# A two-block transformer kernel: the first stage in another order, with the second x tile in two pieces, the tables loaded later and one set of column sums left to TensorE

## The chip, the cores and the metric

The kernel runs on one core of one Trainium2 chip. The metric is the device time of one execution in microseconds (us), as the median of several runs. One more execution is recorded by the profiler; all rows shown are from it.

## The reference, cut to what matters

Two transformer blocks run in a row on 256 tokens of width 2048, in fp32. What the change touches is the start of the first block: the modulation vector, the normed and modulated x, and its product with `w_in`.

```python
cs = jax.nn.silu(c)
mod = cs @ w_ada[l] + b_ada[l]
sh1, sc1, gt1, sh2, sc2, gt2 = [m[:, None, :] for m in jnp.split(mod, 6, axis=-1)]
h = _rmsnorm(x, g_pre_mix[l]) * (1.0 + sc1) + sh1
proj = h @ w_in[l]
p_moba, p_dsa, p_qi, p_ki, p_wi, ga, gb = jnp.split(proj, split_pts, axis=-1)
...
x = x + gt1 * _rmsnorm(y, g_post_mix[l])
h = _rmsnorm(x, g_pre_ffn[l]) * (1.0 + sc2) + sh2
f = jnp.square(jax.nn.relu(h @ w_ff1[l])) @ w_ff2[l]
x = x + gt2 * _rmsnorm(f, g_post_ffn[l])
```

`h` can't be made before the column sums over all 2048 rows of `w_ada` for its columns (`sh1`, `sc1`) are there. The second block (attention with dilated windows and latent attention, then its own feed-forward part) has no modulation and isn't touched.

## The kernel before, in words

**Numbers as pairs.** Every weight is split into a high part `wh` (ScalarE, a copy that rounds, L1307) and a low part `wl` (VectorE, weight minus high part, L1678); `h` is kept as high and low halves in `HT`. One 128x512 product is then three matmuls: high x high (L983), low x high (L984), high x low (L986).

**Chunks.** Weights stream from HBM in the order of `plan()`, one DMA for each event (L930, on SyncE's queue), into seven raw buffers in this stage. An event "g" is a chunk: two rows of 128 of a slab 1024 columns wide. A chunk gives two pieces; `wh` and `wl` have a ring of four pieces, so two chunks. TensorE works a chunk as four banks (ps0 to ps3: two token tiles by two column halves) of six matmuls each, 24 in all.

**Phases.** `h` has 16 column tiles (k = 0 to 15). Six slabs (qi, qB, kB, vB, kA, vA) are run three times, over k 0 to 3, then 4 to 8, then 9 to 15 (`PHASES`). A slab of phase 0 is copied out of PSUM by ScalarE (L1601), one of phase 1 is added by VectorE (L2011). Phase 0 has 12 chunks, called c0 to c11 below, phase 1 has 18.

**Modulations.** Tiles 0, 1 (the first pair) and 2, 3 (the second pair) come from events "p": four events of 1 MB each for a pair, with 256 columns of shift and 256 of scale for four of the 16 rows. TensorE sums the shift columns of such a piece directly (`row_vec`, four matmuls with one output row, L1043), VectorE the scale columns (four operations, L1696 and L1699). After a pair's fourth piece ScalarE copies TensorE's row out (L1353), `column_sums` turns both into columns (L1055, L1058), VectorE forms the modulation `AV` (L1704 to L1711), and `x_halves` writes the two `HT` tiles (ScalarE L1360, VectorE L1761, L1764). The columns for the later phases come as events "s", whose sums VectorE does alone (L1696, L1699); after the last one `column_sums` (L1067) and the tasks "turnx" follow, which scale two tiles of x (ScalarE L1346), turn them (TensorE L1102), apply the modulation (ScalarE L1333, L1337) and make the low half (VectorE L1751).

**Order.** `work_order()` writes one list of items that all engines follow; each engine takes its own kinds from it, in that order. In it the first pair's four sums, its tiles, the second pair's sums and chunk c0 (qi, k 0 and 1) are written by hand; from c1 on `run()` goes through the slabs: the sums of the events behind a chunk, the split of the next chunk, then the four banks. A "rot" task (sines and cosines from the table in `CT`, L1868 to L1900) runs in five parts on VectorE between the first chunks.

**Loads.** SyncE's queue brings the vectors, both token tiles of x (1 MB each) and then the stream; GpSimd's queue brings at the start the constants `CT` (identity and tables, 376 KB), the positions and a mask (192 KB).

```python
def x_norm():
    for t in range(2):
        e.wait_ge(x_landed[t], 16)
```

Of the kernel before, what the change touches and what calls it, by code (L numbers as in the profile page):

```python
# [15 lines left out]
D = 2048  # L16
# [70 lines left out]
def plan():  # L87
# [30 lines left out]
    out += [("p", 0, i) for i in range(4)] + [("p", 1, 0), ("p", 1, 1), chunks.pop(0), ("p", 1, 2), ("p", 1, 3)]  # L118
    beside(chunks, columns, (1, 2, 2, 1, 2, 2, 2, 2, 2, 1, 1))
    beside(phase(1), columns, (1, 1, 1, 1, 1, 1, 1, 1, 1, 1, 1, 1, 1, 1, 0, 0, 0, 0))  # L120
# [143 lines left out]
def work_order():  # L264
# [7 lines left out]
    def add(*item):  # L272
        items.append(item)
# [267 lines left out]
    def first_sums(*ns):  # L541
        for n in ns:
            ada(n)
            add("rowvec", n)
            if n == 0:
                add("xnorm")
                add("xturn", 0)
                add("xturn", 1)

    first_sums(0, 1, 2, 3)  # L550
    add("rowcopy", 3)
    colsum(3)
    first_sums(4)
    add("xhalves", 0)
    split(6)
    first_sums(5, 7, 8)
    for t in range(2):
        for b in range(2):
            if (t, b) == (1, 1):
                add("rowcopy", 8)  # L560
                colsum(8)
            add("bank", "qi@0", parts[6], t, b, True, False)
    at["done"] = parts[6][-1]
    add("xhalves", 1)
    at["pos"] = 9
    later("rot")
    for q in range(2):
        for name in FIRST:
            if (name, q) == ("vA", 0):
                finish("rot")  # L570
            run(f"{name}@{q}", begin=1 if (name, q) == ("qi", 0) else 0)
# [69 lines left out]
def build(nc, stream, vecs, rows, consts, masks, x_in, pos_in, out):  # L641
# [32 lines left out]
    PB, PTB, FIRST_ROW = ACC[:, 1024:1408], ACC[:, 1408:1792], ACC[0:1, 512:768]  # L674
# [15 lines left out]
    vec_in, const_in, caus_in = sem("vec_in"), sem("const_in"), sem("caus_in")  # L690
    x_landed = [sem(f"x{t}_in") for t in range(2)]
# [218 lines left out]

    def x_part(p, t):
# [7 lines left out]
    def sync(e):  # L919
        e.dma_start(VT[:, :], vecs).then_inc(vec_in, 16)  # L920
        for t in range(2):
            e.dma_start(X[:, t, :], x_in[0, 128 * t:128 * t + 128, :]).then_inc(x_landed[t], 16)
        for n, (off, w) in enumerate(offs):
            i, _, m = place[n]
            if m >= 0:
                if events[m][0] == "p":
                    e.wait_ge(*rowvec(m))
                e.wait_ge(*read_last(m))
# [10 lines left out]
    def gpsimd(e):  # L939
        e.dma_start(CT[:, :], consts).then_inc(const_in, 16)  # L940
# [1281 lines left out]
```

## Time and profile before

| | |
|---|---|
| median of three runs | 2619.52 us (2616.36 to 2620.04) |
| the profiled execution | 2613.94 us, span 2612.1 us |
| TensorE busy | 2557.7 us of the span (98%) |
| VectorE, ScalarE busy | 1734.9 us (66%), 1206.0 us (46%) |
| HBM traffic | 216 GB/s over the span, 370 to 376 GB/s in the first 130 us |

The span is what the trace covers; the execution takes 1.8 us more. Busy time of TensorE is modelled from pipelined matmuls, so its idle gaps and the distance between matmul starts say more than its share. The change lies within the first 190 us, so the rows below are mostly of these. A row's bracket gives the engine's idle time before it and what ended that.

### The profile page before, as it was taken

The page shows a single profiled execution, that of the slowest core. Times are in us where ns is not written, and L with a number is a line of the kernel's source. Part 1 is how long each engine was busy: PE and PEld are TensorE (multiplying, and loading weights), DVE is VectorE, ACT ScalarE, POOL GpSimd, SP SyncE. Part 2 cuts the span into 40 slices and gives each one's busy share as a digit, 9 for nine tenths or more (in the row PEclk, how much of TensorE's full clock was granted, in tenths as well). Part 3 has the DMA queues.
Part 4 walks back from the last instruction along what each step waited for, and adds up shares of the span by engine and source line. Part 5 has one row for each costly group of instructions (what it writes and reads, how often), then busy time and mean ns, then how long its engine had stood idle before and what let it go on. Part 6 is the DMA issues. An engine that isn't in the chain of part 4 may idle for free.

```text
span 2612.1 us, 30557 instructions
## 1 busy us (share of the span) xinstructions
PE 2557.7 (98%) x12370; PEld 2115.0 (81%) x12370; DVE 1734.9 (66%) x2307; ACT 1206.0 (46%) x1737; POOL 5.9 (0%) x15
## 2 busy tenths in 40 slices
PE   7999998999999999999999999999999999999998
PEld 4887786887787888888888878878788888888887
DVE  6887878878887776556556564546665565564665
ACT  4534444533446434434434465455564343443443
POOL 0000000000000000000000000000000000000000
PEclk9999999999999999999999999999999999999999
DMA  9984345688885775555555545534545555555553
GB/s 376 375 330 170 121 159 210 265 339 327 338 329 205 292 280 207 199 187 188 199 179 192 195 169 183 189 126 146 185 169 193 181 190 195 188 196 194 178 193 145
DMA packets 80444, 567.11 MB, mean 217 GB/s; under 512 B 8976, under 2 KB 9104, under 8 KB 15664
## 3 DMA queue, kind: packets, MB, share of 16 engines
q1 hardware_dynamic: 79200, 558.09, 58.2%
q0 software_dynamic: 1104, 7.07, 0.7%
q8 instruction: 98, 1.61, 0.2%
q14 instruction: 42, 0.34, 0.0%
HBM read 563.02 MB, written 2.10 MB: 216 GB/s over the span
## 4 chain that ended last, share of the span: by engine, by line
PE 84%; DVE 10%; ACT 2%; DMA 2%; issue 1%; DVEq 0%; SPq 0%; ACTq 0%
PE ps L986 19%; PE ps L983 19%; PE ps L984 18%; PE ps L1027 16%; PE ps L1029 8%; DVE wl L1678 3%; DMA raw<-stream_in 2%; DVE ACC L1699 2%; ACT wh L1307 1%; PE ps L1247 1%; DVE TMP L1804 1%; DVE M L1808 1%; PE ps L1223 1%; DVE M L2011 0%; PE ps L1087 0%
## 5 line engine op out<-in xcount | busy, mean ns | idle before, releaser
L1678 DVE TENSOR_TENSOR wl<-raw,wh 128x1024 fp32r<-128x1024 f32 x845 | 996.7, 1220 | 566.7 <-ACT wh L1307 566.1
L1307 ACT ACTIVATE wh<-raw 128x1024 fp32r<-128x1024 f32 x845 | 846.8, 1049 | 723.3 <-PE ps L986 551.8
L1027 PE MATMUL ps<-HT,wh 128*128 128x512 f32 x1792 | 634.2, 399 | 0.0
L983 PE MATMUL ps<-wh,U 128*128 128x512 f32 x1376 | 538.2, 391 | 0.0
L986 PE MATMUL ps<-wl,U 128*128 128x512 f32 x1376 | 536.4, 390 | 1.3 <-DVE wl L1678 1.3
L984 PE MATMUL ps<-wh,U 128*128 128x512 f32 x1376 | 535.6, 389 | 0.0
L1029 PE MATMUL ps<-HT,wl 128*128 128x256 f32 x1792 | 503.5, 281 | 0.6 <-DVE wl L1678 0.6
L983 PE MATMUL ps<-wh,HT 128*128 128x512 f32 x1096 | 439.0, 401 | 7.7 <-DVE HT L2106 3.3
L986 PE MATMUL ps<-wl,HT 128*128 128x512 f32 x1096 | 432.8, 395 | 11.2 <-DVE wl L1678 11.1
L984 PE MATMUL ps<-wh,HT 128*128 128x512 f32 x1096 | 429.4, 392 | 0.0
L1027 PEld LDWEIGHTS ps<-HT,wh 128*128 128x128 f32 x1792 | 336.6, 188 | 82.7 <-DVE M L2048 0.2
L1029 PEld LDWEIGHTS ps<-HT,wl 128*128 128x128 f32 x1792 | 338.5, 189 | 2.0 <-DVE wl L1678 1.5
L986 PEld LDWEIGHTS ps<-wl,U 128*128 128x128 f32 x1376 | 258.3, 188 | 57.9 <-DVE wl L1678 3.9
L984 PEld LDWEIGHTS ps<-wh,U 128*128 128x128 f32 x1376 | 258.4, 188 | 53.1 <-issue 0.2
L983 PEld LDWEIGHTS ps<-wh,U 128*128 128x128 f32 x1376 | 258.3, 188 | 53.0 <-issue 0.2
L986 PEld LDWEIGHTS ps<-wl,HT 128*128 128x128 f32 x1096 | 207.1, 189 | 63.9 <-DVE wl L1678 20.1
L983 PEld LDWEIGHTS ps<-wh,HT 128*128 128x128 f32 x1096 | 207.5, 189 | 55.0 <-DVE HT L2106 4.5
L984 PEld LDWEIGHTS ps<-wh,HT 128*128 128x128 f32 x1096 | 207.6, 189 | 41.3 <-issue 0.5
L1699 DVE SCALAR_TENSOR_TENSOR ACC<-raw,VT,ACC 128x1024 f32<-128x1024 f32 (+3 forms) x180 | 222.7, 1237 | 5.0 <-DMA raw<-stream_in 0.9
L1617 ACT ACTIVATE M<-ps 128x256 f32<-128x256 f32 x112 | 43.1, 385 | 213.7 <-PE ps L1029 213.7
L1619 ACT ACTIVATE U<-M 128x256 fp32r<-128x256 f32 x112 | 46.8, 418 | 139.3 <-DVE M L2054 139.3
L2048 DVE TENSOR_TENSOR M<-ps,M 128x256 f32<-128x256 f32 x112 | 47.5, 424 | 61.6 <-ACT M L1617 61.1
(265 smaller groups left out, 1373.4 us busy)
## 6 DMA issues: line engine op xcount, KB each, us to landing
raw<-stream_in SPq DMA_DIRECT2D x497, 1024.0 KB, 4.8
raw<-stream_in SPq DMA_DIRECT2D x16, 896.0 KB, 7.4
raw<-stream_in SPq DMA_DIRECT2D x17, 640.0 KB, 6.2
raw<-stream_in SPq DMA_DIRECT2D x13, 512.0 KB, 4.8
M<-rows_in POOLq DMA_DIRECT2D x6, 1024.0 KB, 5.7
X<-x_in SPq DMA_DIRECT2D x2, 1024.0 KB, 7.0
y_out<-X SPq DMA_DIRECT2D x4, 512.0 KB, 2.7
CT<-consts_in POOLq DMA_DIRECT2D x1, 376.0 KB, 6.7
```

Of the source, the lines that this page charges most:

```text
L983: e.matmul(o, ah, H[:, c:c + bw], start=k == k0, stop=False)
L984: e.matmul(o, al, H[:, c:c + bw], start=False, stop=False)
L986: ins = e.matmul(o, ah, L[:, c:c + bw], start=False, stop=end)
L1027: e.matmul(o[:, :], H[:, c], a.rearrange("p h n -> p (h n)"), start=k == 0, stop=False)
L1029: ins = e.matmul(o[:, 0:256], L[:, c], a[:, 0, :], start=False, stop=k == 15)
L1223: e.matmul(bank[7][:, 0:256], att_in(A, "v", h, 0), PTB[:, 0:256], start=True, stop=False)
L1307: e.activation(H, raw[place[n][0]][:, c:c + w], ACT.Copy).then_inc(*hi.tick(p))
L1617: e.activation(z, bank[i % 4][:, 256:512], ACT.Copy).then_inc(*evac_a.tick((name, i)))
L1619: e.activation(d[:, 0, :], z, ACT.Copy).then_inc(*high.tick(key))
L1678: e.tensor_tensor(L, raw[place[n][0]][:, c:c + w], H.bitcast(F32), ALU.subtract).then_inc(*lo.tick(p))
L1699: e.scalar_tensor_tensor(a, r, cs, a, ALU.mult, ALU.add).then_inc(*acc.tick(key))
L2048: e.tensor_tensor(z, p[:, 0:256], z, ALU.add).then_inc(*evac_v.tick((name, i)))
```

## The change

1. **Slab order.** qi@0 holds only k 0 and 1 (one chunk), and qi@1 holds k 2 to 8. So phase 0 has 11 chunks and phase 1 has 19. The chunk of qi@0 is streamed before the second pair's modulations, and qB's first chunk between their second and third piece. Below, c0, c1, ... are the chunks in their order in the kernel at hand, with 24 matmuls each in phase 0 in both.
2. **Hand-written start.** The new list puts c0's four banks and c1's first banks between the second pair's row sums. `x_halves` is done half by half across both engines: the tiles lie in two banks (ps5, ps6), so that ScalarE reads one while VectorE reads the other.
3. **x in pieces.** Token tile 0 of x comes first, tile 1 in two pieces of 512 KB behind the third and the fourth stream event; each tile has its own squares, root and reciprocal.
4. **Tables late.** GpSimd's queue loads only the identity (128 of 752 columns of `CT`) at the start, and the rest and the mask after the second pair's last row sum. VectorE's rot and rope wait for `table_in`.
5. **One piece by TensorE alone.** For event ("p", 1, 0) TensorE sums all 512 columns, and VectorE none; `column_sums` adds that part.
6. **Columns.** The 32 "s" events are spread otherwise: 16 over phase 0's chunks c2 to c10, 16 over phase 1's first 16 chunks (before: 18 and 14).

```diff
+SLABS["qi@0"], SLABS["qi@1"] = (*SLABS["qi"][:3], 0, 2), (*SLABS["qi"][:3], 2, PHASES[2])
...
-    out += [("p", 0, i) for i in range(4)] + [("p", 1, 0), ("p", 1, 1), chunks.pop(0), ("p", 1, 2), ("p", 1, 3)]
-    beside(chunks, columns, (1, 2, 2, 1, 2, 2, 2, 2, 2, 1, 1))
+    out += [("p", 0, i) for i in range(4)] + [chunks.pop(0), ("p", 1, 0), ("p", 1, 1), chunks.pop(0), ("p", 1, 2), ("p", 1, 3)]
+    beside(chunks, columns, (1, 2, 2, 2, 2, 2, 2, 2, 1))
...
+    add("xsquare", 0)
+    add("xnorm", 0)
+    for n in range(3):
+        sums(n)
...
+    add("xsquare", 1)
+    sums(3)
+    add("xsquare", 2)
     add("rowcopy", 3)
...
+    add("xturn", 0)
+    split_piece(4, 0, only=("ACT",))
     add("xhalves", 0)
...
+    add("bank", "qi@0", parts[4], 0, 0, True, True)
+    evac("qi@0", 0, 0)
+    sums(5, False)
+    add("bank", "qi@0", parts[4], 0, 1, True, True)
+    add("xturn", 1)
+    evac("qi@0", 0, 1)
+    sums(6)
+    split(7)
...
+    add("bank", "qB@0", parts[7], 0, 0, True, False)
+    for n in (8, 9):
+        sums(n)
+    add("rowcopy", 9)
...
+    def both_by_pe(n):
+
+        return events[n] == ("p", 1, 0)
...
-        for t in range(2):
-            e.dma_start(X[:, t, :], x_in[0, 128 * t:128 * t + 128, :]).then_inc(x_landed[t], 16)
+        e.dma_start(X[:, 0, :], x_in[0, 0:128, :]).then_inc(x_landed[0], 16)
         for n, (off, w) in enumerate(offs):
+            if n in (3, 4):
+                a = slice(1024 * (n - 3), 1024 * (n - 3) + 1024)
+                e.dma_start(X[:, 1, a], x_in[0, 128:256, a]).then_inc(x_landed[n - 2], 16)
...
-        e.dma_start(CT[:, :], consts).then_inc(const_in, 16)
+        e.dma_start(CT[:, 0:C_COS], consts[:, 0:C_COS]).then_inc(const_in, 16)
         e.dma_start(POS[:, :], pos_in).then_inc(pos_landed, 16)
+        e.memset(ONES[:, :], 1.0).then_inc(ones_set, 1)
+        e.wait_ge(*rowvec(9))
+        e.dma_start(CT[:, C_COS:C_N], consts[:, C_COS:C_N]).then_inc(table_in, 16)
...
+                w = 512 if both_by_pe(n) else 256
```

**First place, TensorE behind the first pair.** ps4 takes the row sums (`L1043` before, `L1081` now), ps5 and ps6 the turned x, ps0 to ps3 the chunk's banks. Before, right behind the first pair's column sums:

```order
L1058 MATMUL ps7<-ONES,ACC 128x1 x2
L1043 MATMUL ps4<-raw4,VT 1x256 x4
L1043 MATMUL ps4<-raw5,VT 1x256 x4
L1043 MATMUL ps4<-raw0,VT 1x256 x4
L1043 MATMUL ps4<-raw1,VT 1x256 x4
L983 MATMUL ps0<-wh0,HT 128x512
```

The same place now, from the last turned tile of the first pair:

```order
L1148 MATMUL ps6<-CT,RT 128x128
L1019 MATMUL ps0<-wh0,HT 128x512
L1020 MATMUL ps0<-wh0,HT 128x512
L1022 MATMUL ps0<-wl0,HT 128x512
L1019 MATMUL ps0<-wh1,HT 128x512
L1020 MATMUL ps0<-wh1,HT 128x512
L1022 MATMUL ps0<-wl1,HT 128x512
L1081 MATMUL ps4<-raw5,VT 1x512 x4
L1019 MATMUL ps1<-wh0,HT 128x512
```

The first bank of c0 moved ahead of all four row sums of the second pair, and one of these is twice as wide. In what follows there (not shown) ps1, a turn of x, the next row sum, ps2, ps3, c1's ps0, two row sums, c1's ps1, the column sums and c1's ps2 and ps3 come in this order.

**Second place, ScalarE between phase 0 and phase 1.** `M<-ps` copies a bank out, QKT and RT take scaled x, `TMP<-ps5` and `TMP<-ps6` apply the modulation to a turned pair of tiles. Before, from the split of the last chunk of phase 0 (c11):

```order
L1307 ACTIVATE wh3<-raw1 128x1024
L1346 ACTIVATE QKT<-X,RS 128x256
L1346 ACTIVATE RT<-X,RS 128x256
L1333 ACTIVATE TMP<-ps5,AV 128x256 x2
L1337 ACTIVATE HT<-TMP 128x2x256
L1307 ACTIVATE wh0<-raw3 128x1024
L1307 ACTIVATE wh1<-raw3 128x1024
L1601 ACTIVATE M<-ps0 128x512
L1601 ACTIVATE M<-ps1 128x512
L1346 ACTIVATE QKT<-X,RS 128x256
```

Now, from the last copy of phase 0:

```order
L1654 ACTIVATE M<-ps3 128x512
L1394 ACTIVATE QKT<-X,RS 128x256
L1394 ACTIVATE RT<-X,RS 128x256
L1384 ACTIVATE TMP<-ps5,AV 128x256 x2
L1388 ACTIVATE HT<-TMP 128x2x256
L1394 ACTIVATE QKT<-X,RS 128x256
L1394 ACTIVATE RT<-X,RS 128x256
L1384 ACTIVATE TMP<-ps6,AV 128x256 x2
L1388 ACTIVATE HT<-TMP 128x2x256
L1355 ACTIVATE wh0<-raw2 128x1024
L1355 ACTIVATE wh1<-raw2 128x1024
L1394 ACTIVATE QKT<-X,RS 128x128
```

Two tiles' worth of work now stands in one piece behind phase 0's last bank. On TensorE (not shown) the column sums L1110 x10 and the eight turns L1148 into ps5 and ps6 stand directly behind that bank too, and ahead of the first bank of c11, the first chunk of phase 1; before, the ten column sums stood ahead of c10, the turns into ps5 in the middle of c10 and those into ps6 in the middle of c11.

## Rows read from the trace of the kernel before

**Rows 1.** Windows by stage; columns PE, PEld, DVE, ACT, POOL busy (x), clock, DMA, GB/s.

```profile
12.67:42.45 29.78, 25.73 (x113) 12.99 (x113) 21.15 (x49) 8.74 (x16) 0.00 (x0) 1.00 1.01 421
...
51.26:94.79 43.53, 43.53 (x194) 36.05 (x193) 42.55 (x45) 26.56 (x35) 0.00 (x0) 1.00 0.98 384
94.79:123.90 29.11, 27.72 (x135) 22.61 (x134) 21.55 (x22) 19.14 (x29) 0.00 (x0) 1.00 0.90 354
123.90:166.07 42.17, 41.93 (x184) 34.07 (x184) 42.17 (x37) 15.26 (x15) 0.00 (x0) 1.00 0.97 374
...
183.59:2612.10 2428.51, 2393.94 (x11638) 1989.21 (x11637) 1583.76 (x2124) 1119.06 (x1623) 3.73 (x7) 1.00 0.56 205
```

**Rows 2.** Timeline of the start (start, us, engine, line, operation, count, idle before).

```profile
6.55 1.91 ACT L1312 ACTIVATE M<-X 128x2048 f32<-128x2048 f32 x1 [3.70 <-DMA X<-x_in]
17.63 2.05 DVE L1699 SCALAR_TENSOR_TENSOR ACC<-raw,VT,ACC 128x256 f32<-128x256 f32 x4 [0.43 <-DMA raw<-stream_in]
23.23 0.37 ACT L1353 ACTIVATE ACC<-ps 1x256 f32<-1x256 f32 x1 [6.39 <-PE ps L1043]
27.57 2.00 ACT L1307 ACTIVATE wh<-raw 128x1024 fp32r<-128x1024 f32 x2 [1.20 <-DMA raw<-stream_in]
28.89 2.35 DVE L1678 TENSOR_TENSOR wl<-raw,wh 128x1024 fp32r<-128x1024 f32 x2
```

**Rows 3.** TensorE, fp32 matmuls: two pieces' row sums; ns min/median/max at 512 columns.

```profile
24.79 3.61 PE L1043 MATMUL ps<-raw,VT 128*1 128x256 f32 x16
...
L1075 PE MATMUL ps<-ACC,ONES x16: 590/592/595, 595.5 to 1003.4; 128*128 128x512 f32 x16
```

**Rows 4.** Timeline, ScalarE: the copy of c1's last bank.

```profile
51.46 0.60 ACT L1601 ACTIVATE M<-ps 128x512 f32<-128x512 f32 x1 [0.76 <-PE ps L986]
```

**Rows 5.** Timeline, VectorE between c2 and c5.

```profile
46.30 2.35 DVE L1678 TENSOR_TENSOR wl<-raw,wh 128x1024 fp32r<-128x1024 f32 x2
48.57 0.16 DVE L1868 CAST ST<-POS 128x2 f32<-128x2 int32 x1
...
50.70 3.21 DVE L1699 SCALAR_TENSOR_TENSOR ACC<-raw,VT,ACC 128x1280 f32<-128x1280 f32 x2
...
61.85 0.20 DVE L1878 TENSOR_SCALAR M<-M 128x96 f32<-128x96 f32 x1
...
63.34 1.55 DVE L1699 SCALAR_TENSOR_TENSOR ACC<-raw,VT,ACC 128x1280 f32<-128x1280 f32 x1
```

**Rows 6.** Timeline, three engines from phase 0 to phase 1.

```profile
94.79 2.29 PE L1067 MATMUL ps<-ONES,ACC 128*128 128x1 f32 x20
96.94 0.48 PE L983 MATMUL ps<-wh,HT 128*128 128x512 f32 x1
97.46 1.15 DVE L1696 TENSOR_SCALAR ACC<-raw,VT 128x1792 f32<-128x1792 f32 x1
...
106.39 0.50 ACT L1346 ACTIVATE QKT<-X,RS 128x256 f32<-128x256 f32 x1
106.94 0.33 PE L1102 MATMUL ps<-CT,QKT 128*128 128x128 f32 x1 [1.08 <-ACT QKT L1346]
107.92 1.02 ACT L1333 ACTIVATE TMP<-ps,AV 128x256 f32<-128x256 f32 x2 [0.64 <-PE ps L1102]
108.97 0.63 ACT L1337 ACTIVATE HT<-TMP 128x512 fp32r<-128x512 f32 x1
110.67 0.60 ACT L1601 ACTIVATE M<-ps 128x512 f32<-128x512 f32 x1 [0.58 <-PE ps L986]
```

**Rows 7.** Timeline: phase 1, first addition on VectorE; TensorE's last column sums.

```profile
123.90 2.48 DVE L2011 TENSOR_TENSOR M<-ps,M 128x512 f32<-128x512 f32 x4
...
180.55 3.18 PE L1067 MATMUL ps<-ONES,ACC 128*128 128x1 f32 x28
```

**Rows 8.** Window at the lower clock, columns as in rows 1.

```profile
44.50:47.90 3.40, 3.40 (x8) 2.47 (x9) 3.40 (x4) 1.24 (x2) 0.00 (x0) 0.54 0.72 251
```

**Rows 9.** DMA issues: KB, us to landing.

```profile
CT<-consts_in POOLq DMA_DIRECT2D x1, 376.0 KB, 6.7
```

More of the change, by code:

```diff
@@ L539, in ffn, with sums @@
                 later("srow", f)
[L541 to L550, printed above, removed]
+    def sums(n, dve=True):
+        if dve:
+            add("ada", n)
+        add("rowvec", n)
+    add("xsquare", 0)
+    add("xnorm", 0)
+    for n in range(3):
+        sums(n)
+    for p in range(2):
+        add("xq", p, 0)
+    add("xsquare", 1)
+    sums(3)
+    add("xsquare", 2)
     add("rowcopy", 3)
+    add("xnorm", 1)
+    add("xq", 0, 1)
     colsum(3)
-    first_sums(4)
+    add("xturn", 0)
+    split_piece(4, 0, only=("ACT",))
     add("xhalves", 0)
-    split(6)
-    first_sums(5, 7, 8)
-    for t in range(2):
[L558 to L563, printed above, removed]
-    add("xhalves", 1)
-    at["pos"] = 9
+    add("DVE", "split", parts[4][0])
+    split_piece(4, 1)
+    add("xq", 1, 1)
+    add("bank", "qi@0", parts[4], 0, 0, True, True)
[6 more added lines that the diff above has]
+    split(7)
+    for b in range(2):
+        add("bank", "qi@0", parts[4], 1, b, True, True)
+        evac("qi@0", 1, b)
+    at["done"] = parts[4][-1]
+    add("bank", "qB@0", parts[7], 0, 0, True, False)
+    for n in (8, 9):
+        sums(n)
+    add("rowcopy", 9)
+    add("bank", "qB@0", parts[7], 0, 1, True, False)
+    split_piece(10, 0)
+    colsum(9)
+    add("xhalves", 1)
+    split_piece(10, 1)
+    for b in range(2):
+        add("bank", "qB@0", parts[7], 1, b, True, False)
+    at["done"] = parts[7][-1]
+    at["pos"] = 10
     later("rot")
@@ L570, in work_order @@
                 finish("rot")
-            run(f"{name}@{q}", begin=1 if (name, q) == ("qi", 0) else 0)
+            if (name, q) != ("qi", 0):
+                run(f"{name}@{q}", begin=1 if (name, q) == ("qB", 0) else 0)
         flush()
@@ L1096, in x_turn @@
             e.wait_ge(const_in, 16)
-            for s, q in free[b]:
-                e.wait_ge(*s(q))
+            for q0 in ((5, 6) if p < 2 else (b,)):
+                for s, q in free[q0]:
+                    e.wait_ge(*s(q))
             for i in range(nk):
@@ L1352, in row_copy @@
             e.wait_ge(*rowvec(n))
[L1353 removed]
+            e.activation(FIRST_ROW[:, 0:w], bank[4][0:1, 0:w], ACT.Copy).then_inc(*copied.tick(("row", n)))
         def x_halves(p):
@@ L1364, in turn_x @@
         def turn_x(task, seg):
-            x_turn(task[1])
             k = X_TILES[task[1]][0]
+            e.wait_ge(*turned(("turnx", task[1] - 2)))
+            for t in range(2):
+                x_quarter(task[1], t)
             e.wait_ge(*mods(("av", 1, max(q for q in PHASES if q <= k))))
```

108 lines of the change are left out of this document (62 added, 46 removed).

## The prediction

> **What bounds the kernel now.** I read three views, in this order: the windows by stage, to see which engine is full in each; the timeline of the first 50 us, to see what TensorE waits for; and the timeline around the step from phase 0 to phase 1, where the order of work changes again.
>
> The windows [rows 1] show five stages. From 12.67 to 42.45 us TensorE has only 113 matmul records, and DMA is full (1.01) at 421 GB/s. From 51.26 to 94.79 both TensorE and VectorE are full (43.53 and 42.55 of 43.53 us) and DMA nearly (0.98). From 123.90 to 166.07 VectorE is busy for 42.17 of 42.17 us: it sets the pace there. After 183.59 TensorE is busy 2394 of 2429 us and VectorE 1584, and nothing in the change touches this part. So what counts is how much earlier or later TensorE stands at the same point of its work at about 184 us; that shift goes through to the end one to one.
>
> Units. The eight chunks c2 to c9 run from 51.26 us (c1's last copy starts at 51.46 [rows 4], about 0.2 us behind the bank's last start) to the column sums at 94.79 [rows 6]: 5.44 us a chunk, 0.227 us a matmul. A stream event of 1 MB takes 2.48 us: the third lands at 17.63, the seventh at 27.57 [rows 2], so the first landed at 12.67.
>
> **The start, until c2 begins.** Ahead of the first event x's second tile goes (1 MB, 2.48 us) and the tables and the mask (0.50 MB, 1.2 us), so it lands at 8.97. The fourth lands at 17.65 behind the first half tile, the second half tile at 18.9, c0's weights at 21.4, and the second pair's four pieces and c1's at 23.9, 26.3, 31.3, 33.8 and 28.8. Loads then run 1.2 us ahead of before, event for event.
>
> When does c0's first bank end? The half tile's squares take about 1.1 us (half of 1.91 [rows 2], and a read-out), so ScalarE copies the row at 20.05. Before, 5.66 us lay between that copy and the split of c0 (23.23 to 28.89), of which 2.0 were four sums that no longer stand between (2.05 for four [rows 2]); the turn of x is now inside the stretch (0.7, from 106.94 and what follows it in [rows 6]). So `wl` starts at 24.4, both pieces are there 2.27 us later (46.30 to 48.57 [rows 5]), and the first bank ends at 26.95. Bounds: 24.7 (c0's landing, one copy and the two splits, nothing else) and 29.
>
> From there TensorE has no wait that I can find until c2, since everything it needs has landed before its turn. It has 42 matmuls of c0 and c1 (9.5 us); three row sums at 1.71 (two take 3.4 without the tail of 3.61 [rows 3]); the wide row sum of the piece that it sums alone, 3.4; a turn, 0.7; six narrow column sums at 0.215 (ten take 2.15, from 94.79 to 96.94 [rows 6]), 1.3. The wide one isn't in the trace of before in this form: its lower bound is 1.71 (width free), the upper 4.7 (eight records one behind the other at the 592 ns of the fp32 matmul of 512 columns [rows 3]); I take 3.4, double width at double time, nearest to the narrow row that it widens. Sum: 20.0 us, so **c2 begins at 47.1 instead of 51.26, 4.2 us earlier**. 2.0 us of VectorE's work is saved for 1.7 of TensorE's, in a stretch where VectorE will wait (about 9 us between 28.8 and 44) and TensorE won't; the 1.7 is in the sum.
>
> **Phase 0.** VectorE finishes c2's split at about 48.0, and from there works in one piece. Its load per chunk is a split 2.27 and two columns 3.12 (the row at 50.70 has 3.21 with its tail [rows 5]), 5.39 against TensorE's 5.44, plus the rot parts: 2.13 behind c3's split (48.57 to 50.70 before), 1.49 in the third part (61.85 to 63.34), 0.2 for each small operation (61.85), so 0.4 in each of the others. Before, single columns at c1 and c4 made room for these; now there is one, 0.8 us for the first form. From 48.0: 0.8; split, rot, two columns 7.52; 5.75; 6.88; and 1.13 for the first half of c6's split: 70.1. TensorE wants it at 47.1 + 4 x 5.44 + 0.46 = 69.3. So 0.8 late, and 0.3 more at c7 and at c8, each behind a small rot part: **1.4 us given back**. Phase 0's 11 chunks end at T = 47.1 + 9 x 5.44 + 1.4 = 97.5.
>
> **From phase 0 to phase 1.** Here two tiles of x are now made in a row with no chunk between. Column sums take until T+2.15; the modulation is there at T+2.7 (96.94 to 97.46), ScalarE's two applications and copy end at T+4.4 (1.02 + 0.63), only then comes the scaling for the second tile, and TensorE's turn starts 0.55 later (106.39 to 106.94 [rows 6]) and ends at T+5.65: c11 starts. The second tile's application starts 1.53 behind its scaling (106.39 to 107.92), T+5.9, and ends at T+7.6; ScalarE then does c12's two copies, 2.0 (27.57 [rows 2]), and the third tile's scaling, so the turn in the middle of c11 is at T+10.1, when its first two banks are done since T+8.4. c12 starts at T+13.1 = 110.6. Before, c12 started at 110.47 (110.67 less 0.2) with the third tile's turn, 0.6, still in front; c13 at 116.5 against 116.0 now. So **of 2.8 us left, 2.3 go here** and 0.5 stay.
>
> **Phase 1.** VectorE's cadence is 42.17 / 3 = 14.06 us a slab [rows 1]: five splits, three columns, four additions from 123.90 on [rows 7]. TensorE needs 60 x 0.227 = 13.6. The 0.5 us is kept through three slabs. But kA's slab had two columns before, its column sums coming at 180.55 [rows 7], and has three now: a fourth slab at VectorE's pace, 0.45 slower. The column sums (about 3 us) are the same and only one chunk later; the turns behind them have 5 us and more of chunks each in front of their use. **Shift at the end: 0.1 us earlier, so none.**
>
> Costed at nothing: the tables late (0.50 MB in a stretch where the loads are ahead: c4's weights land about 46, ScalarE takes them at 53; rival three has the price), the pieces of x (one more reduction and one more addition on VectorE while it waits), the two-bank `x_halves` (its saving of half a us is within the bounds of the first bank).
>
> The profiled execution took 2613.94 us, its span 2612.1 and 1.8 around it; less 0.1 it is 2613.8. The median shown is 5.6 above the profiled one, so the forecast on its scale is **2619.4**.
>
> **Rival one, the start's gain goes through.** If the boundary costs what it cost before, and phase 0 keeps TensorE's pace, 4.2 less 0.45 stay: 2615.8. For it: VectorE is idle for 8.6 of the 29.78 us up to 42.45 and for 7.6 of the 29.11 behind 94.79 [rows 1], so there is slack on both sides of phase 0. Against it: ScalarE's order puts two tiles behind phase 0's last bank, and TensorE's turn waits for the second's scaling. A part of it is likelier than all.
>
> **Rival two, the low clock (slower).** In 44.50 to 47.90 the granted clock was 0.54 and TensorE started 8 matmuls in 3.4 us [rows 8], 0.425 apiece, which is the 1.2 GHz level; such a stretch costs 1.6 us. It came behind a gap at the end of c0. Now the gap there is gone, which is in my 4.2. But the first bank of c0 stands between waits at 22 to 27 us, and the boundary has a wait of 2.8 us behind narrow column sums. One stretch at the boundary costs nothing, as the third tile's turn leaves TensorE 1.7 us idle inside c11. In the start it costs 1.6 each, up to three (each followed by new waits on narrow sums): 2621.1 for one, 2624.3 for three; from the fourth the change is slower by over 0.2%.
> The Trainium skill (TensorE: Matmul & The Clock Gate, Part 4: PE-mode transpose) says that turns on TensorE don't count as busy for the clock as other matmuls do. By that rule the eight turns ahead of c11 make the low stretch there near certain; the sum would be the same, as it lies in c11. No row here shows it.
>
> **Rival three, the tables come too late (slower).** Their load waits for the last row sum, about 41.7. Before, 376 KB took 6.7 us from issue to landing [rows 9] among full queues; so 48.4, and VectorE needs them behind c3's split at 51.1: 2.7 us of cover. If they take twice as long (13.4), VectorE stands still for 4.0 us in a stretch where it sets the pace: 2623.4; slower than before from about 9.5 us on.
> The Trainium skill (SBUF — State Buffer, section "A bandwidth-pool intuition that's wrong") says a load from GpSimd's queue can be held up by VectorE operations that take the shared port, and gives 3.1 us for one that takes 0.6 alone. With 2.5 us more the tables would land at 50.9, just in time, and the sum would stand.
>
> **How the numbers follow.** No change, within 1.5 us of 2619.4: 0.50. Rival one in part or whole, 2615 to 2618: 0.27. Rival two: 0.17. Rival three: 0.06. The start's bounds (first bank 24.7 to 29, wide sum 1.7 to 4.7) move c2 by 4 us down and 3.4 up, but phase 0 and the boundary give most of it back in the same way; half of it I count at the end. Medians of three here spread by 1 to 2 us besides. The range is 2614.0 to 2623.5. A change of 0.2% is 5.2 us, about what a measurement of this kernel can tell from none. Faster by more needs rival one whole and the low stretch or the first bank at its bound too: 0.06. Slower by more needs three to four low stretches or very late tables: 0.07. So 0.87 for the same.
>
> **What would show it.** In the profile of the changed kernel: c0's first matmul at about 24 and c2's at 47; VectorE idle for 8 to 9 us between 28 and 44; TensorE waiting for `wl` at c6 by under 1 us; a wait of TensorE of about 2.5 us for ScalarE's scaling (QKT or RT, L1394) near 100 us and one of about 1.6 near 107; VectorE's first addition (L2074) at 123.4; the second column sums about at the same time as before plus one chunk. I am wrong if c11 starts before 101 us, if VectorE isn't the full engine in phase 1, or if a clock of 0.5 shows before 47 us.

## The result, and the profile after

| | kernel before | changed kernel |
|---|---|---|
| median | 2617.74 us (20 runs, 2614.53 to 2622.59) | 2622.22 us (20 runs, 2619.03 to 3191.05) |
| the profiled execution | 2613.94 us, span 2612.1 | 2621.33 us, span 2619.5 |

The change makes the kernel slower: ratio 1.0015, 95% interval 1.0008 to 1.0022, so about 4 us. One run of 3191.05 us was disturbed and is left out of the ratio. The forecast was "no change" (0.1 us earlier) at 2619.4 us. The time lies in its range, but the step is small and real: the interval's lower end is above 1.

The windows of the changed kernel (columns: PE, PEld, DVE, ACT, POOL busy with counts, clock, DMA share, GB/s). The first four are stages, laid out like those of [rows 1]: the start up to the end of c0's first bank, phase 0 from c2 on, the step between the phases (from the column sums behind c10 to VectorE's first addition), and three slabs of phase 1.

```profile
9.61:28.25 18.64, 14.48 (x50) 5.98 (x50) 13.55 (x32) 7.95 (x16) 0.00 (x0) 0.91 1.01 423
49.51:100.85 51.34, 50.43 (x217) 40.09 (x216) 49.19 (x58) 29.66 (x40) 0.00 (x0) 1.00 0.94 366
100.85:127.16 26.31, 24.09 (x111) 19.59 (x110) 17.21 (x17) 14.99 (x23) 0.00 (x0) 0.87 0.84 323
127.16:169.34 42.18, 41.95 (x184) 34.08 (x184) 42.18 (x38) 15.26 (x15) 0.00 (x0) 1.00 0.96 364
24.80:28.20 3.40, 3.15 (x6) 1.59 (x6) 3.33 (x6) 0.69 (x2) 0.00 (x0) 0.50 1.01 422
103.30:110.10 6.80, 4.58 (x15) 3.33 (x13) 1.97 (x6) 5.13 (x10) 0.00 (x0) 0.50 0.65 268
192.10:198.90 6.80, 6.80 (x21) 5.53 (x21) 1.54 (x4) 0.00 (x0) 0.00 (x0) 0.50 0.43 142
```

The last three rows are stretches at the low clock: 0.50 of 2.4 GHz is the 1.2 GHz level. In the trace of before there was one such stretch from 20 to 180 us [rows 8] and one of 3.4 us behind the last column sums, at 184.7. Now there is one over c0's first bank, one over the step between the phases, and one of 6.8 us behind the last column sums.

The timeline of the start and of c6 (start, us, engine, operation, idle before), to be laid beside [rows 2, 4]. L1019, L1020 and L1022 are the three matmuls of a product, L1081 the row sums:

```profile
19.69 1.06 ACT L1361 ACTIVATE M<-X 128x1024 f32<-128x1024 f32 x1 [2.70 <-DMA X<-x_in]
24.78 0.79 PE L1019 MATMUL ps<-wh,HT 128*128 128x512 f32 x1 [1.93 <-DVE HT L1827]
24.98 2.35 DVE L1733 TENSOR_TENSOR wl<-raw,wh 128x1024 fp32r<-128x1024 f32 x2
28.25 3.59 PE L1081 MATMUL ps<-raw,VT 128*1 128x512 f32 x8
39.93 3.61 PE L1081 MATMUL ps<-raw,VT 128*1 128x256 f32 x16
49.51 0.39 PE L1019 MATMUL ps<-wh,HT 128*128 128x512 f32 x1
72.83 0.50 PE L1022 MATMUL ps<-wl,HT 128*128 128x512 f32 x1 [0.71 <-DVE wl L1733]
```

c2 begins at 49.51, 1.75 us earlier than the 51.26 before. The step between the phases, to be laid beside [rows 6]:

```profile
100.85 2.29 PE L1110 MATMUL ps<-ONES,ACC 128*128 128x1 f32 x20
103.18 0.17 DVE L1759 TENSOR_TENSOR AV<-ps,VT 128x5 f32<-128x5 f32 x1 [3.24 <-PE ps L1110]
103.92 1.02 ACT L1384 ACTIVATE TMP<-ps,AV 128x256 f32<-128x256 f32 x2 [1.48 <-DVE AV L1766]
105.50 0.49 ACT L1394 ACTIVATE QKT<-X,RS 128x256 f32<-128x256 f32 x1
106.05 0.47 PE L1148 MATMUL ps<-CT,QKT 128*128 128x128 f32 x1 [2.22 <-ACT QKT L1394]
107.00 0.78 PE L1019 MATMUL ps<-wh,HT 128*128 128x512 f32 x1
127.16 2.48 DVE L2074 TENSOR_TENSOR M<-ps,M 128x512 f32<-128x512 f32 x4
```

T, the start of the column sums behind phase 0, is 100.85, c11 starts at 107.00, and VectorE's first addition comes at 127.16 instead of 123.90 [rows 7]. A wait of TensorE for an addition, 1.4 us long and at the same point of the work in every kernel here, serves as a mark near 300 us:

```profile
297.01 0.50 PE L983 MATMUL ps<-wh,HT 128*128 128x512 f32 x1 [1.39 <-DVE M L2011]
```

```profile
302.69 0.50 PE L1019 MATMUL ps<-wh,HT 128*128 128x512 f32 x1 [1.39 <-DVE M L2074]
```

The first is the kernel before, the second the changed one: 5.7 us late. Behind it the order of work is the same in both. The spans differ by 7.4 at the end; the other 1.7 is one stretch of low clock at 1943 us that only the second trace has. Such stretches vary from run to run (next section).

### The profile page after: what moved, and what is told of

Same layout as the page of the kernel before. It is cut to its first block, busy times and chain, and to the rows that moved or that the text cites. A ratio compares the mean times of both kernels' runs of the same rounds, so it can differ in the third digit from the quotient of the medians.

```text
span 2619.5 us, 30569 instructions
## 1 busy us (share of the span) xinstructions
PE 2567.7 (98%) x12374; PEld 2118.1 (81%) x12374; DVE 1733.4 (66%) x2306; ACT 1206.1 (46%) x1740; POOL 6.4 (0%) x16
## 4 chain that ended last, share of the span: by engine, by line
PE 85%; DVE 10%; ACT 2%; issue 1%; DMA 1%; SPq 0%; DVEq 0%; ACTq 0%
PE ps L1022 19%; PE ps L1019 19%; PE ps L1020 19%; PE ps L1063 16%; PE ps L1065 8%; DVE wl L1733 3%; DVE ACC L1754 2%; ACT wh L1355 1%; PE ps L1295 1%; DMA X<-x_in 1%; DVE TMP L1867 1%; DVE M L1871 1%; PE ps L1271 1%; DVE M L2074 1%; PE ps L1110 0%
## 5 line engine op out<-in xcount | busy, mean ns | idle before, releaser
L1019 PE MATMUL ps<-wh,U 128*128 128x512 f32 x1376 | 538.2, 391 | 0.0
L1022 PE MATMUL ps<-wl,U 128*128 128x512 f32 x1376 | 536.4, 390 | 1.4 <-DVE wl L1733 1.4
L1020 PE MATMUL ps<-wh,U 128*128 128x512 f32 x1376 | 535.5, 389 | 0.0
L1019 PE MATMUL ps<-wh,HT 128*128 128x512 f32 x1096 | 440.2, 402 | 8.7 <-DVE HT L2169 3.3
L1022 PE MATMUL ps<-wl,HT 128*128 128x512 f32 x1096 | 433.7, 396 | 10.7 <-DVE wl L1733 10.7
L1020 PE MATMUL ps<-wh,HT 128*128 128x512 f32 x1096 | 430.6, 393 | 0.0
L1022 PEld LDWEIGHTS ps<-wl,U 128*128 128x128 f32 x1376 | 258.3, 188 | 57.8 <-DVE wl L1733 3.8
L1020 PEld LDWEIGHTS ps<-wh,U 128*128 128x128 f32 x1376 | 258.4, 188 | 53.3 <-issue 0.2
L1019 PEld LDWEIGHTS ps<-wh,U 128*128 128x128 f32 x1376 | 258.3, 188 | 52.9 <-issue 0.2
L1022 PEld LDWEIGHTS ps<-wl,HT 128*128 128x128 f32 x1096 | 207.6, 189 | 66.4 <-DVE wl L1733 22.5
L1019 PEld LDWEIGHTS ps<-wh,HT 128*128 128x128 f32 x1096 | 208.0, 190 | 57.4 <-DVE M L2074 4.9
L1020 PEld LDWEIGHTS ps<-wh,HT 128*128 128x128 f32 x1096 | 208.0, 190 | 41.2 <-issue 0.5
```

Of the source, the lines that this page charges most:

```text
L1019: e.matmul(o, ah, H[:, c:c + bw], start=k == k0, stop=False)
L1020: e.matmul(o, al, H[:, c:c + bw], start=False, stop=False)
L1022: ins = e.matmul(o, ah, L[:, c:c + bw], start=False, stop=end)
```

## The experiments

Twelve kernels were measured in three groups of four, each group on a chip of its own and together with the kernel before. The first group is the two same kernels again, one_tile and fill_boundary; the second fill_start, no_wide, spread and tables_early; the third light_fill and the three combinations. Times are medians; the kernel before had 2617.69 in the first group, 2618.28 in the second, 2618.05 in the third. Within a group medians can be set side by side. Between groups only the ratios to the kernel before can, and a difference of 0.001 (2.6 us) between two ratios is about what their intervals leave open. So the times say whether a kernel is faster than the one before, and the traces what one part of it cost.

### The same two kernels again

No edit.

> The changed kernel once more, for its clock: if the low stretches (24.8 to 28.2, 103.3 to 110.1, 192.1 to 198.9, two near 440, one at 1943 us) belong to the order of work, the first three stand in the same places again and last as long; if they are chance, they move or change in number. Time 2622 in either case, 0.15% over the kernel before.

> The kernel before once more, for its clock: low stretches at 44.5 to 47.9 and 184.6 to 188.0 again if they belong to the order of work, each 3.4 us long; ratio 1.000.

The changed kernel: 2621.74 us, ratio 1.0015 (1.0006 to 1.0024). The kernel before: 2615.90, ratio 0.9996 (0.9985 to 1.0006). Windows of the changed kernel's second trace, then of the other's:

```profile
24.40:31.70 7.30, 6.05 (x11) 2.12 (x12) 5.24 (x9) 2.31 (x4) 0.00 (x0) 0.55 1.01 422
105.90:113.30 7.40, 5.80 (x16) 4.54 (x17) 3.44 (x4) 6.05 (x12) 0.00 (x0) 0.54 0.46 189
193.90:198.00 4.10, 4.10 (x17) 3.32 (x17) 1.54 (x4) 0.00 (x0) 0.00 (x0) 0.61 0.22 48
```

```profile
44.70:48.20 3.50, 3.16 (x8) 2.44 (x8) 3.50 (x5) 1.58 (x3) 0.00 (x0) 0.52 0.68 231
```

The places belong to the order of work; the lengths don't. In the start the low clock lasted 3.4 us in one trace and about 7 in the other, and behind the last column sums 6.8 and 3.4. Further stretches, near 430, 450, 720 or 1940 us, come and go in both kernels.

The execution of the second trace of the kernel before took 2623.78 us, 10 more than that of the first, though it had passed the mark at 297.49, only 0.5 later. About 3 of the 10 are two more stretches of low clock (at 434 and 1946 us). Most of the rest, 6 to 7 us, is not the clock: near 730 us weights came late in this trace and TensorE waited for them. The first row is the trace before at this place, the second the later one; clock 1.00 in both, DMA share 0.99 and 0.73:

```profile
722.00:734.00 12.00, 12.00 (x57) 9.91 (x56) 11.46 (x11) 4.62 (x5) 0.00 (x0) 1.00 0.99 373
728.00:742.00 14.00, 11.31 (x44) 7.50 (x43) 10.56 (x9) 4.50 (x5) 0.00 (x0) 1.00 0.73 245
```

Why they came late isn't shown. So shifts are read at the mark and verdicts from the timed runs.

### The step between the phases: one_tile

```diff
-        finish("turnx", X_TILES.index((PHASES[q + 1], 2)))
+        if q:
+            finish("turnx", X_TILES.index((PHASES[q + 1], 2)))
```

> The changed kernel, but at the step from phase 0 to phase 1 only the column sums stand between c10 and c11; the turns of the two x tiles come in the middle of c11 and of c12, as in the kernel before (the work is the same, only its place). Theory W (the wait for ScalarE's scaling, 2.2 us, and the turns behind it, not covered by any chunk, are what the boundary costs, and what runs slowly behind them follows from that): c11 starts about 2.2 us behind the end of c10 instead of 6.15, so TensorE is 3.9 us earlier, less up to 1 us for a wait of c12 for its tile: VectorE's first addition at 124 instead of 127.2, and the kernel 3 to 4 us faster than the changed one, about 2618.5, level with the kernel before. Theory G (VectorE is the bound right behind the boundary, so whatever TensorE gains there it gives back in phase 1): first addition within 1 us of 127.2 and the time within 1 us of the changed kernel, 2622. Theory K (the low clock comes behind the column sums whatever follows them): a stretch at clock 0.5 still stands at about 103 to 110 us, now over the matmuls of c11, costs 1.7 to 3.4 us there and eats most of the gain: 2620 to 2621.

2619.44 us, ratio 1.0008 (1.0000 to 1.0017): 2.3 less than the changed kernel in the same group. The window from T to the first addition:

```profile
102.48:125.54 23.06, 22.85 (x115) 18.62 (x113) 17.13 (x18) 15.17 (x24) 0.00 (x0) 1.00 0.96 364
```

23.06 us against 26.31 (26.48 in the second trace): 3.3 saved, at clock 1.0, for the same work. Theory W holds. Theory G falls: VectorE is busy for only 17.13 of it. Theory K falls in this trace, but not for good: in four of the eight later kernels with this step (no_wide, spread, light_fill, combo_parts) a stretch of 3.4 us stood there, and T to the first addition took 24.6 us instead of 23.0. So where chunks cover the step a stretch at the low clock costs its full 1.6, and the new place of the turns is worth 1.7 to 3.3 us. The first addition came at 125.54, not at the expected 124, since c2 began 1.65 us later in this trace than in the first one of the changed kernel.

### The wait filled: fill_boundary

```diff
-        finish("turnx", X_TILES.index((PHASES[q + 1], 2)))
+        if q:
+            finish("turnx", X_TILES.index((PHASES[q + 1], 2)))
+        else:
+            steps(1)
+            add("PE", "fill", parts[at["pos"]][0], 2, 9)
+            steps(1)
```

> The changed kernel with nine extra matmuls of 128x512 (c11's first wh piece against h, into an unused bank, never read; about 2.0 us at full clock) on TensorE between the turns of the first and of the second x tile at the boundary, where it waits 2.2 us for ScalarE. They do nothing else. Theory W: the wait is what costs; filled or not, c11 starts at the same time (107.0 in the trace's time, up to 0.5 later), the time is that of the changed kernel or up to 1 us more. Theory K2 (TensorE's idle time at the boundary brings the second 3.4 us of low clock over c11's matmuls): the granted clock is 1.0 again when c11 starts, its first eight matmuls take 0.227 us each instead of 0.43, and the kernel is 1.4 to 1.7 us faster than the changed one: 2620.6. If the low clock comes from the narrow column sums alone, the stretch from 103.3 on stays, the nine matmuls run in it at 0.43 each (3.8 us), and the kernel is 1.5 to 2 us slower than the changed one.

2622.67 us, ratio 1.0017 (1.0008 to 1.0026), as the changed kernel. Two windows of it, and the turn in the middle of c11:

```profile
103.30:110.10 6.80, 6.56 (x33) 4.87 (x33) 2.04 (x6) 5.08 (x10) 0.00 (x0) 1.00 0.75 308
101.44:127.21 25.77, 24.23 (x120) 19.78 (x119) 17.21 (x18) 14.99 (x23) 0.00 (x0) 1.00 0.85 321
```

```profile
111.45 0.30 PE L1162 MATMUL ps<-CT,QKT 128*128 128x128 f32 x1 [1.30 <-ACT QKT L1410]
```

The clock stayed at 1.0, yet T to the first addition took 25.77 instead of 26.31 to 26.48: the 6.8 us of low clock were worth 0.5 to 0.7 us, not K2's 1.4 to 1.7. At the full clock TensorE waits 1.30 us inside c11 for the third tile's scaling; in the changed kernel there is no such wait, as the slow matmuls ahead of it take up the time. The other 2.7 us against one_tile's 23.06 are the two tiles in a row: the wait for the scaling, and the turns that no chunk covers. One trace can't say whether filling always keeps the clock.

### The start filled: fill_start and light_fill

Both are one_tile with fp32 matmuls of 128x512 that compute nothing, in TensorE's waits ahead of c0. light_fill has four: one behind the third row sum, one behind the fourth, two behind the first turns. fill_start has nine, at these places and behind the first two row sums as well. Of light_fill's edit:

```diff
+    add("PE", "fill", 1)
...
     sums(3)
+    add("PE", "fill", 1)
...
     add("xturn", 0)
+    add("PE", "fill", 2)
...
+        def fill(count):
...
+            for _ in range(count):
+                e.matmul(bank[3][:, :], ONES[:, :], X[:, 0, 0:512], start=True, stop=True)
```

> The kernel one_tile with nine extra fp32 matmuls of 128x512 on TensorE (ones against x, into a bank that c0 overwrites later; 0.59 us each), where TensorE waits in the start: one behind each of the first two row sums, three behind the third, one behind the fourth, three behind the first turns. They compute nothing. In one_tile's trace the granted clock is 0.5 from about 24.4 to 31.5 us, over c0's first bank and the wide row sum. Theory K (the low clock comes behind TensorE's waits and narrow sums in the start, and costs what it slows there): with the waits filled the clock stays 1.0 until phase 0, c0's first bank ends about 0.6 us sooner, the wide sum takes 3.6 instead of 4.8 us, c2 begins 1.8 us or more earlier, and the kernel is 1.5 to 2.5 us faster than one_tile: 2617.5. Theory G2 (VectorE is the bound in phase 0 and 1, so an earlier start is given back): c2 earlier as above, but the first addition within 0.5 us of one_tile's 125.5 and the time 2619.4. If the fillings delay c0 or the clock falls all the same: 2620 or more.

> The kernel one_tile with four extra fp32 matmuls of 128x512 in TensorE's waits in the start (one behind the third row sum, one behind the fourth, two behind the first turns; they compute nothing). In fill_start nine of them, 0.93 us each as its trace showed, took the low clock out of the start but put c0 off by 2.75 us, so that c2 came 0.9 us later. Theory K: four fit in the waits, the clock stays 1.0 over c0, c0's first matmul comes at most 0.3 us later than in one_tile, c2 1.7 to 1.9 us earlier, and the kernel is 1.5 to 2 us faster than one_tile: 2617.5 to 2618. Rival: four don't keep the clock up; a stretch at 0.5 stands at 24 to 32 us as before and the time is one_tile's, 2619.4.

fill_start: 2618.62 us, ratio 1.0009 (1.0000 to 1.0017), against 1.0008 for one_tile: no gain. light_fill: 2616.50, ratio 0.9990 (0.9981 to 0.9999). The same window of one_tile and of light_fill:

```profile
24.40:31.70 7.30, 6.21 (x11) 2.10 (x12) 5.08 (x9) 2.15 (x4) 0.00 (x0) 0.54 1.01 420
```

```profile
24.40:31.70 7.30, 6.28 (x16) 1.85 (x16) 4.71 (x8) 1.81 (x3) 0.00 (x0) 1.00 1.01 421
```

Sixteen matmul records instead of eleven in the same 7.3 us. The wide row sum takes 4.80 us in one_tile and 3.59 in light_fill. From the start of c0's two low parts (25.44 in one_tile, 25.04 in light_fill) to the end of its first bank, where the wide sum begins, it is 3.28 and 2.84 us, so the low clock costs that bank 0.44:

```profile
25.44 2.35 DVE L1734 TENSOR_TENSOR wl<-raw,wh 128x1024 fp32r<-128x1024 f32 x2
28.72 4.80 PE L1082 MATMUL ps<-raw,VT 128*1 128x512 f32 x8
52.91 0.60 ACT L1655 ACTIVATE M<-ps 128x512 f32<-128x512 f32 x1
```

```profile
25.04 2.35 DVE L1745 TENSOR_TENSOR wl<-raw,wh 128x1024 fp32r<-128x1024 f32 x2
27.88 3.59 PE L1085 MATMUL ps<-raw,VT 128*1 128x512 f32 x8
50.87 0.60 ACT L1666 ACTIVATE M<-ps 128x512 f32<-128x512 f32 x1
```

The last row of each is the copy of c2's first bank: 2.0 us earlier in light_fill, 0.6 of it from an earlier first landing (9.44 against 10.06) and 1.4 from the clock (0.44 and 1.2, less 0.2 by which the fills put c0 off).

Theory K holds for c2. G2 falls for phase 0: from c2's first copy to T both take 49.6 us. At the mark, though, light_fill's trace is only 0.45 us ahead (298.98 against 299.43), since it had one of the 1.6 us stretches at the step between the phases, which one_tile's had not. That the fills gain time at the end rests on the timed runs: 0.9990 against 1.0008 between two groups, and, in one group, combo 3.2 us under combo_nofill (below). fill_start had the full clock too but put c0 off by 2.75 us, as the expectation of light_fill tells; I had sized a fill at 0.59 us when it takes two such records, 0.93.

### The wide row sum: no_wide

```diff
-    sums(5, False)
+    sums(5)
...
-        return events[n] == ("p", 1, 0)
+        return False
...
-                part = events[n][1] == 1
+                part = False
```

> The kernel one_tile with VectorE summing the scale columns of the second pair's first piece again, and TensorE's row sum of it 256 wide. My prediction counted the wide sum as 1.7 us on TensorE's path against 2.0 us of VectorE's that wait anyway. By that, c2 begins 1.7 us earlier (if VectorE does the four extra operations in its idle 5.9 us before 35), the kernel is up to 1.7 us faster than one_tile, 2617.7. Rival: VectorE's four operations stand ahead of c1's split or of the copy that the modulation waits for, and the gain is under 0.5 us; or phase 0 gives it back: c2 earlier, first addition the same.

2618.21 us, ratio 0.9995 (0.9985 to 1.0006), 1.0008 for one_tile in the group before; the intervals overlap. From the end of c0's first bank to c2's first copy one_tile took 28.83 to 52.91, 24.08 us; no_wide 22.41:

```profile
29.36 0.60 ACT L1655 ACTIVATE M<-ps 128x512 f32<-128x512 f32 x1 [2.88 <-PE ps L1023]
...
51.77 0.60 ACT L1655 ACTIVATE M<-ps 128x512 f32<-128x512 f32 x1
```

1.67 less, with about 7 us of low clock in the start of both. That this is the 1.7 counted is chance, as the low clock fell on the row sum that stands behind c0's first bank in both: it took 4.73 us wide and 3.50 narrow. At the full clock, in combo and light_fill, the same stretch takes 20.56 and 22.88 us, 2.3 apart: 1.7 for the row sum (3.53 against 1.82) and 0.6 for the two extra column sums, which the prediction's price of the wide piece left out. The rivals fall: VectorE had the time, and phase 0 took its 49.6 us as in one_tile. In the traces this part of the change is a loss of 1.7 to 2.3 us.

### The columns: spread

```diff
-    beside(chunks, columns, (1, 2, 2, 2, 2, 2, 2, 2, 1))
+    beside(chunks, columns, (1, 2, 2, 1, 2, 2, 2, 2, 2))
```

> The kernel one_tile with one column sum of VectorE (1.55 us) moved from behind c5 to behind c10, so that c5 has one and c10 two. The prediction had VectorE late for c6, c7 and c8 (traces: TensorE loses 1.4, 0.3 and 0.3 us there). If that is what phase 0 loses, c6 has no wait, T (the end of c10) is 1.4 to 2 us earlier against c2, and the kernel is 1 to 2 us faster: 2618. Rival: VectorE's total work is the bound up to the first additions; then the 2 us come back as a wait of c11 or of the first additions (2.3 instead of 0.9 us there), and the time is that of one_tile, 2619.4.

2615.53 us, ratio 0.9989 (0.9980 to 0.9997), more than the 1 to 2 us expected. Between c2 and T TensorE loses no more than 0.3 us for `wl`, at c8. In this kernel's trace the low clock lasted 13.6 us in the start, so its mark near 300 us tells little:

```profile
20.40:34.00 13.60, 11.04 (x27) 4.96 (x26) 7.78 (x19) 6.14 (x11) 0.00 (x0) 0.50 1.02 423
```

The saving is read behind it: from c2's first copy to T it is 49.6 us in one_tile and in no_wide (51.77 to 101.37), and 47.9 to 48.0 in spread, combo_nofill and combo: 1.6 less. The rival falls: from T to the first addition it is 23.0 us in one_tile, combo_nofill and combo alike. By the ratios (0.9989 against 1.0008, two groups) the gain would be 5 us, by the medians 3.9; the traces show only 1.6 of it.

### The tables: tables_early

```diff
-        e.wait_ge(*rowvec(9))
         e.dma_start(CT[:, C_COS:C_N], consts[:, C_COS:C_N]).then_inc(table_in, 16)
```

> The kernel one_tile with the rest of the tables and the mask (0.50 MB) loaded at the start, as before the change, instead of behind the second pair's last row sum. If the late tables bought what their bytes say, the stream's events land 1.2 us later from the first on, c0's first bank ends 1.2 us later and, as TensorE is full from there, the kernel is up to 1.2 us slower than one_tile: 2620.6. Rival: the landing of the second half tile and of c0's weights isn't what c0 waits for, or the start's low clock moves with it, and the time is within 0.5 us of one_tile's.

2620.43 us, ratio 1.0011 (1.0001 to 1.0021); one_tile had 1.0008. By the timed runs the two can't be told apart. In the traces c0's first matmul is at 26.33 instead of 25.24, and the wide sum, 4.80 us in one_tile, falls wholly into the low clock:

```profile
29.80 5.51 PE L1081 MATMUL ps<-raw,VT 128*1 128x512 f32 x8
```

So c2 comes 1.8 us later, 1.1 by the bytes (1.2 counted) and 0.7 by the clock, and the first addition too (127.31 instead of 125.54). Loading the tables late costs nothing that a row shows: in the changed kernel VectorE starts the first operation of "rot" at 53.64, right behind the split ahead of it.

### All of it: combo_nofill, combo, combo_parts

combo_nofill is one_tile with spread and no_wide; combo adds light_fill's four matmuls; combo_parts is combo with the last column sums cut in four parts, one behind each bank of that chunk (of its edit):

```diff
+                        for m in due:
+                            if events[m][:2] == ("s", 2):
+                                add("PE", "colpart", m, 4 * (2 * t + b), 4 * (2 * t + b) + 4)
```

> one_tile with both single changes that its offspring tried: VectorE's column sum moved from c5 to c10 (spread) and the wide row sum taken back (no_wide). Their traces gave 1.6 us in phase 0 and 1.7 us in the start. If both are on the path: c2 at about 50, T about 99.5, and a time 1.5 to 3.3 us below one_tile: 2616 to 2618, at or under the kernel before. If VectorE's total is the bound, the two overlap (the wide sum spares VectorE four operations, 1.9 us, that it now has to do) and the time is that of the better one alone.

> combo_nofill with light_fill's four matmuls. Theory K: a further 1.7 us from the full clock over c0: first addition 1.5 to 2 us earlier than in combo_nofill, time 2614.5 to 2616.5, under the kernel before by about 0.1%. If VectorE is the bound between c2 and the first addition the 1.7 us are given back there and the two are level.

> combo with the 28 records of narrow column sums at the end of phase 1 (3.0 us in one piece) cut into four parts that stand behind the four banks of that chunk. A low stretch of 3.4 us or more came 3 us behind that piece in eight of the ten traces so far, 1.6 us each. If the piece brings it, the stretch is gone and the kernel is up to 1.6 us faster than combo; if it is chance or comes from something else, the stretch stays in most runs and the time is combo's.

| | median | ratio to the kernel before |
|---|---|---|
| combo_nofill | 2614.51 us | 0.9988 (0.9977 to 0.9999) |
| combo | 2611.34 us | 0.9974 (0.9964 to 0.9984) |
| combo_parts | 2611.85 us | 0.9972 (0.9960 to 0.9984) |

combo's windows, by the same four stages as those of the changed kernel:

```profile
9.92:28.32 18.40, 16.59 (x58) 6.45 (x58) 13.14 (x31) 7.86 (x16) 0.00 (x0) 1.00 1.02 423
47.25:96.93 49.68, 49.66 (x218) 40.23 (x217) 48.45 (x58) 29.67 (x40) 0.00 (x0) 1.00 0.97 375
96.93:119.92 22.99, 22.78 (x115) 18.62 (x113) 17.88 (x19) 15.28 (x24) 0.00 (x0) 1.00 0.98 398
119.92:162.08 42.16, 41.09 (x179) 33.40 (x180) 42.16 (x37) 15.08 (x15) 0.00 (x0) 1.00 0.96 369
```

combo beats both kernels: 6.7 us under the kernel before, and by the ratios (0.9974 and 1.0015) about 11 under the changed one. Its mark is at 292.19, 4.8 earlier than before. Two of the three came out below the range expected of them: combo_nofill by 1.5 us, though its trace had 13.6 us of low clock in the start and T at 101.1 instead of 99.5, and combo by 3.2. So a sum of parts that were measured one at a time is good to about 3 us here, and no better. combo's start had no low clock; its median is 3.2 us under that of combo_nofill, with intervals of the ratios that just overlap. combo_parts is level with combo, and combo too had no stretch behind its uncut column sums (nor had fill_start and no_wide), so whether the cut prevents one stays open.

```profile
292.19 0.50 PE L1023 MATMUL ps<-wh,HT 128*128 128x512 f32 x1 [1.40 <-DVE M L2086]
```

## Why the prediction was wrong

The step that failed is the sum for the start: c2 was to begin at 47.1 and began at 49.51 in the first trace of the changed kernel and at 51.2 in the second. The steps behind it were sound in kind, each a little short. This is how far each stage was off, in us, with both traces set against the first trace of the kernel before, from which the prediction was made:

| | first trace | second trace |
|---|---|---|
| start, to c2 | 2.4 | 4.1 |
| phase 0, c2 to T | 1.0 | 0.9 |
| step, T to the first addition | 0.4 | 0.6 |
| phase 1, to the mark | 2.0 | 0.3 |
| sum | 5.8 | 5.9 |

The forecast at the mark was 0.1 earlier, and the marks (302.69 and 302.86, against 297.01) are 5.7 and 5.85 later: the sums close.

- **The start.** Of the 2.4 us, 0.6 are the loads: the first landed at 9.61, not 8.97, and c0's split into low parts began at 24.98, not 24.4. 0.4 is the low clock over c0's first bank (3.27 us from the start of the split, 2.84 in light_fill), and 0.3 the bank's end behind its split, which was given too little at the full clock too. The last 1.1 is TensorE's work from there to c2, 21.26 us instead of the 20.15 used, with the clock at 1.0. Set against the terms of the forecast, which add up to 20.0: the wide sum 3.53 (I took 3.4, right), the three narrow ones 5.4 instead of 5.1, the column sums 1.6 instead of 1.3, the turn 0.5 instead of 0.7, and 0.7 more for the 42 matmuls, of which each first one behind a narrow piece takes 0.33. In the second trace c0's first bank ended 0.6 later still, with the loads, and the low clock also covered the wide sum, 4.56 us instead of 3.53:

```profile
28.88 4.63 PE L1081 MATMUL ps<-raw,VT 128*1 128x512 f32 x8
33.44 0.50 PE L1019 MATMUL ps<-wh,HT 128*128 128x512 f32 x1
```

- **How much of it is the clock.** Of the sums of 5.8 and 5.9 the low clock makes up about 2.6 us in the first trace (0.4 in the start, 0.5 at the step, and 1.65 behind the last column sums, where the stretch was twice as long as before) and 2.2 in the second (1.5 in the start, 0.7 at the step), so somewhat under half. The rest is work and loads that I sized too small.
- **Phase 0, forecast 1.4 given back, measured 2.4** (51.34 less nine chunks of 5.44). Right in mechanism: TensorE lost 1.4 at c6 instead of 0.8, and 0.3 each at c7 and c8, the waits for `wl` where they were forecast; another 0.2 went at c2's own first `wl`. spread removes most of them.
- **The step between the phases, forecast T + 5.65 for c11 and T + 25.9 for the first addition, measured T + 6.15 and T + 26.31.** Right, with the wait for ScalarE's scaling of 2.22 near 106. fill_boundary, at the full clock, has 25.77 and the second wait near 111 (1.30, forecast about 1.6). The first addition came 3.8 later than my 123.4, nearly all of it by T's 3.35.
- **The low clock there, forecast to cost nothing.** It cost 0.5 to 0.7 (fill_boundary). The rule of the Trainium skill that the prediction named (TensorE: Matmul & The Clock Gate, Part 4: PE-mode transpose) made a stretch here near certain. The traces agree as far as they go: both of the changed kernel have one over the turns (0.50 and 0.54 in the windows above), and the one with wide matmuls between the turns has none. They don't single out the turns, since narrow sums and a wait stand there too.
- **Phase 1, forecast 14.06 a slab for four slabs, 0.45 lost.** Right: additions follow each other in 14.06 (127.16, 141.22, ... 183.39). From the first addition to the mark the changed kernel took 173.88 in its second trace against 173.11 before, with one stretch of low clock of 3.4 us in each: 0.77 lost. In the first it took 175.53, as its stretch was twice as long, another 1.65.
- **Rival two** had one of the causes, at 0.17, and its price of 1.6 a stretch was right where TensorE is full (1.65 in phase 1, 1.6 at the step in light_fill); in the start of the changed kernel the low clock cost 0.4 and 1.5. Its time for one stretch, 2621.1, is near the measured 2622.2, but partly by luck: the terms that were sized too small aren't in it. What the prediction didn't count was how TensorE would stand ahead of its new first wide matmul: three waits, of 1.05, 0.93 and 1.93 us, between row sums, column sums and turns up to 24.8 us.
- **Rival one** fell. So did **rival three**: the "rot" work ran from 53.64 on without a wait for the tables.
- **"I am wrong if a clock of 0.5 shows before 47 us"** came true. c11 didn't start before 101, and VectorE was full in phase 1. VectorE's idle time between 28 and 44 us was 8.9, as forecast.

Two parts of the change, x in pieces and `x_halves` over two banks, were costed at nothing and were not undone in any run, so what they are worth stays open. What the other parts do was shown one at a time on top of one_tile, not on the kernel before, and the medians (4 us slower) and the mark (5.4 to 5.7) agree only within the interval.

## What to carry to other kernels

When work with wide matmuls is moved up between loads, look at what TensorE does in the microseconds ahead of it. Here waits and narrow sums stood there, and the low clock fell on the very matmuls that were brought forward; four matmuls that compute nothing took it away and were worth 1.4 us at c2 in one trace, nearly as much as the whole move (1.75). They must fit in the waits: nine of them gained nothing. Leave a row of small serial tasks (sums, modulation, scaling, turn) where chunks cover them; put together at a step between two phases they cost 1.7 to 3.3 us here, as much as the start had gained or more. And when a sum has a dozen small terms, price each from a row where it stands behind the same neighbour: what the first wide matmul behind a narrow piece, the row sums and the column sums took beyond their estimates came to 1.1 us, a quarter of the gain that was forecast for the start.

## What was not expected of the hardware

- The low clock in the start was there in all eight traces of a kernel with this start and no filling, for 3.4, about 7 or even 13.6 us, and in none of the four with four to nine filling matmuls. The two traces with 13.6 us (spread and combo_nofill) are those with the longest wait ahead of the fourth row sum, 2.25 and 2.49 us; elsewhere it was 0.98 to 1.88. Whether the wait made the difference isn't shown.
- Every trace of either kernel begins at the slow pace: the records of the first row sums (256 columns) start 0.43 us apart, in the changed kernel up to 14.26 us, and 0.215 apart from 14.63 on. The clock column counts this first part as full, so it says too much for windows that begin there. The Trainium skill (TensorE: Matmul & The Clock Gate, Part 1: The HAM clock gate) says that the slow state is the default and that activity releases it; this agrees, and so does light_fill (1.00 in place of 0.54).
- An fp32 matmul of 128x512 appears as two records and takes 0.93 us for both, as against 0.227 for one in the pair format.
- At the same place and behind the same 28 records of column sums the low clock came for 6.8 us, for 3.4 us or not at all.
